# The added row of six gate products, given to TensorE as two rounded parts in a buffer of its own

## What is computed

```
h = rmsnorm_2(x, g_mix[l])
proj = jnp.einsum('bsd,dc->bsc', h, w_in[l])
q_a, k_a, v_a, q_i, k_i, w_i, conv_in, q_m, gate_logits = jnp.split(proj, split_points, axis=-1)
...
gates = jax.nn.sigmoid((gate_logits + b_gate[l]).astype(jnp.float32)).astype(x.dtype)
gates = gates.reshape(B, S, N_BRANCHES, D)
merged = (gates[:, :, 0] * (o_a @ w_br_a[l])
          + gates[:, :, 1] * (o_b @ w_br_b[l])
          + gates[:, :, 2] * (o_m @ w_br_m[l]))
x = x + merged @ w_o[l]
```

## Time and profile before

| | us |
|---|---|
| median of 3 runs | 1756.24 (1755.83 to 1758.96) |
| the profiled execution, its own time | 1757.07 |
| its span, first to last instruction | 1755.0 |
| TensorE busy | 1660.3 |
| VectorE busy | 1216.7 |
| ScalarE busy | 868.3 |
| GpSimd busy | 51.4 |
| mean granted TensorE clock | 0.967 of full |

### The profile page before, as it was taken

How to read it: one execution, slowest core, us unless ns; L and a number is a source line. 1 busy time by engine, 2 the same in 40 slices (tenths; PEclk the granted TensorE clock), 3 DMA queues, 4 the chain that set the end, 5 groups by cost and what they waited for, 6 DMA issues and landing times.

```text
span 1755.0 us, 19937 instructions
## 1 busy us (share of the span) xinstructions
PE 1660.3 (95%) x7889; PEld 1311.8 (75%) x7889; DVE 1216.7 (69%) x1705; ACT 868.3 (49%) x1239; POOL 51.4 (3%) x81
## 2 busy tenths in 40 slices
PE   6999986999999999989999999999989989999997
PEld 2888864778868888658788878766768787787875
DVE  3989976789856765544655555686577558888986
ACT  3445441534444444346544445544354437777774
POOL 1100000001000000000000001000000010000000
PEclk9999997999999999999999999998599989999999
DMA  9998952988749755340666644452022328989993
GB/s 350 375 348 274 323 169 91 360 304 291 249 148 333 251 190 183 133 144 7 235 215 190 193 138 123 162 163 84 26 107 73 120 73 310 353 315 323 333 332 127
DMA packets 200564, 373.78 MB, mean 213 GB/s; under 512 B 8880, under 2 KB 102486, under 8 KB 200464
## 3 DMA queue, kind: packets, MB, share of 16 engines
q1 hardware_dynamic: 186192, 320.48, 53.8%
q0 software_dynamic: 13872, 50.86, 8.3%
q10 hardware_dynamic: 400, 1.10, 0.2%
HBM read 371.36 MB, written 1.05 MB: 212 GB/s over the span
## 4 chain that ended last, share of the span: by engine, by line
PE 84%; DVE 8%; ACT 5%; DMA 1%; issue 1%; SPq 0%; DVEq 0%; ACTq 0%
PE banks L519 23%; PE banks L521 22%; PE banks L520 22%; PE banks L746 2%; PE banks L1258 1%; PE banks L1285 1%; ACT full L718 1%; DVE ul L463 1%; PE banks L1737 1%; PE banks L872 1%; PE banks L2195 1%; PE banks L671 1%; ACT uh L452 1%; PE banks L2240 1%; PE banks L1272 1%
## 5 line engine op out<-in xcount | busy, mean ns | idle before, releaser
L463 DVE TENSOR_TENSOR ul<-raw,uh 128x1024 fp32r<-128x1024 f32 (+2 forms) x548 | 659.6, 1211 | 253.2 <-ACT uh L452 244.9
L452 ACT ACTIVATE uh<-raw 128x1024 fp32r<-128x1024 f32 (+2 forms) x548 | 571.5, 1050 | 488.1 <-PE banks L521 462.5
L519 PE MATMUL banks<-uh,hh 128*128 128x512 f32 (+2 forms) x1280 | 523.5, 409 | 21.8 <-ACT kvm L1123 15.3
L521 PE MATMUL banks<-uh,hl 128*128 128x512 f32 (+2 forms) x1280 | 501.3, 392 | 0.0
L520 PE MATMUL banks<-ul,hh 128*128 128x512 f32 (+2 forms) x1280 | 500.6, 391 | 0.0
L519 PEld LDWEIGHTS banks<-uh,hh 128*128 128x128 f32 x1280 | 244.5, 191 | 85.4 <-ACT kvm L1123 16.2
L520 PEld LDWEIGHTS banks<-ul,hh 128*128 128x128 f32 x1280 | 244.8, 191 | 53.6 <-issue 7.7
L521 PEld LDWEIGHTS banks<-uh,hl 128*128 128x128 f32 x1280 | 244.1, 191 | 51.0
L519 PE MATMUL banks<-uh,bh 128*128 128x512 f32 x528 | 209.3, 396 | 9.3 <-DVE bl L926 4.2
L521 PE MATMUL banks<-uh,bl 128*128 128x512 f32 x528 | 206.0, 390 | 0.0
L520 PE MATMUL banks<-ul,bh 128*128 128x512 f32 x528 | 205.6, 389 | 0.0
(11 more groups left out here) (310 smaller groups left out, 1412.6 us busy)
## 6 DMA issues: line engine op xcount, KB each, us to landing
raw<-in_ffn_w_in SPq DMA_DIRECT2D x176, 512.0 KB, 5.4
raw<-in_w_up SPq DMA_DIRECT2D x64, 1024.0 KB, 5.8
raw<-in_ffn_w_out SPq DMA_DIRECT2D x44, 1024.0 KB, 7.1
arena<-in_ada_w POOLq DMA_DIRECT2D x42, 1024.0 KB, 8.2
raw<-in_w_down SPq DMA_DIRECT2D x32, 1024.0 KB, 5.6
raw<-in_ada_w SPq DMA_DIRECT2D x30, 1024.0 KB, 6.3
raw<-in_w_in SPq DMA_DIRECT2D x22, 1024.0 KB, 5.1
raw<-in_w_mem_kv SPq DMA_DIRECT2D x4, 1024.0 KB, 6.0
```

The source lines that it names most:

```text
L452: act.e.activation(uh[r][:, 0:w], raw[m % NRAW][:, h * w:(h + 1) * w], AF.Copy).then_inc(act_done, ta.put("hi", u))
L463: dve.e.tensor_tensor(ul[r][:, 0:w], raw[m % NRAW][:, h * w:(h + 1) * w], uh[r][:, 0:w].bitcast(F32), ALU.subtract).then_inc(dve_done, tv. ...
L519: pe.e.matmul(o, a, wh, start=s0, stop=False)
L521: mm = pe.e.matmul(o, b, wh, start=False, stop=s1)
```

## The change

GpSimd loads `b_gate` twice, into rows 0 to 5 and 32 to 37 of `adab`. VectorE, in `mix_dve` behind the last low part of the activation (`scaled_dve`), writes a new buffer `gb` of type fp32r: a selecting matrix `gsel` of 38 x 6, zeros, the rounded rows in rows 0 to 5, and in rows 32 to 37 what the rounding left out. `gates_pe` starts each bank with one fp32r matmul over 38 rows, which adds both parts. TensorE no longer waits for the load itself but for VectorE. The second buffer of `pr6` is now `adab`, which is free by then; that makes the arena 516 elements shorter, and `cc` and `st` lose two elements each.

```diff
-ARENA = 11332
+ARENA = 10816
...
-        cc = sb("cc", [P, 48])
+        cc = sb("cc", [P, 46])
...
-        st = sb("st", [P, 280])
+        st = sb("st", [P, 278])
...
+        gb = sb("gb", [P, 520], F32R)
...
-        pr6 = [wide_bufs[2], A(512)]
+        pr6 = [wide_bufs[2], adab[:, :]]
...
+        gsel = gb[0:38, 512:518]
+        gbias = gb[0:38, 0:512]
+
+        def gate_rows_dve(dve):
+            low = gb[32:38, 0:512]
+            dve.wait_ge(loaded("b_gate"), 32)
+            dve.e.tensor_tensor(gsel, ident[0:38, 0:6], ident[0:38, 32:38], ALU.add).then_inc(dve_done, tv.put())
+            dve.e.memset(gb[0:38, 0:512].bitcast(F32), 0.0).then_inc(dve_done, tv.put())
+            dve.own()
+            dve.e.tensor_copy(gbias[0:6, :], adab[0:6, :]).then_inc(dve_done, tv.put())
+            dve.e.tensor_copy(low, adab[32:38, :]).then_inc(dve_done, tv.put())
+            dve.own()
+            dve.e.tensor_tensor(gbias[32:38, :], adab[32:38, :], low.bitcast(F32), ALU.subtract).then_inc(
+                dve_done, tv.put("gb"))
...
-            pe.wait_ge(loaded("b_gate"), 16)
+            pe.wait_ge(dve_done, tv("gb"))
             for b in PAIRS[0]:
                 pe.take(b)
-                pe.e.matmul(PB[b], ident[0:6, j:j + 1].to_broadcast([6, P]), adab[0:6, :], start=True, stop=False)
+                pe.e.matmul(PB[b], gsel[:, j:j + 1].to_broadcast([38, P]), gbias, start=True, stop=False)
...
             scaled_dve(dve, "mix", KD, hh, hl, lambda k: col("g_mix_2", k), lambda k: 0.0)
+            gate_rows_dve(dve)
             dve.e.memset(uT[:, :, 0:30], 0.0).then_inc(dve_done, tv.put("u0"))
...
-            load("b_gate", adab[0:6, :], I["b_gate_2"].rearrange("a (j n) -> (a j) n", n=512))
+            for r in (0, 32):
+                load("b_gate", adab[r:r + 6, :], I["b_gate_2"].rearrange("a (j n) -> (a j) n", n=512))
```

## The result

| | before, us | changed, us |
|---|---|---|
| median | 1755.83 (1752.15 to 1758.96, 5 runs) | 1742.74 (1735.36 to 1743.48, 5 runs) |
| profiled execution, its span | 1757.07, 1755.0 | 1742.52, 1740.7 |
| mean granted TensorE clock of it | 0.967 | 0.971 |

The ratio is 0.9922, 95% interval 0.9896 to 0.9949: faster by 13.1 us at the medians. The prediction said 1744.0, from 1739.5 to 1750.5.

A forecast was written before the change was run, and what follows sets the result against it. TensorE's order was taken as the bound; gains of 3.0 (gates 1 to 3), 4.4 (gate 4), 2.3 (gate 5) and 2.9 (gate 6) sum to 12.6 us, giving 1744 us, 8-in-10 range 1739.5 to 1750.5.

The forecast's parts named there:

- The bound and the path: TensorE holds 84% of the chain that ended last, so time taken from its order is gained unless something replaces it.
- VectorE's five instructions and the load: Near 1074 us: instructions take 2.3 us, hidden while TensorE is busy; the second load lands in time; both cost zero.
- The fp32r pass: Start of each bank: 0.23 us over 38 rows at full clock; a full-clock gate gives 1.2 us.
- Gates 1 to 3: At most 1.8 of 2.4 us reach gate 3 because VectorE holds back the rest; gate 3 adds 1.2: 3.0 us.
- Gate 3's fall: The 3.5 us at half clock behind gate 3, worth 1.7 us, stay because the wait for ScalarE grows.
- Gate 4 and the half clock behind it: At gate 4, shorter passes give 1.7 us and the clock holding behind them 2.7: 4.4 us.
- Gate 5 to gate 6: Gate 5 begins at half clock; passes give 2.9 us, taken as 2.3 since the clock may come back later.
- Gate 6 to the memory heads: Gate 6's passes give 1.2 us and the clock holding behind it 1.7: 2.9 us; VectorE can follow.
- The share of the clock: Of the 12.6 us gain, 4.4 come from the clock holding behind gates 4 and 6, some 8.2 from passes.
- A second HAM failure mode: psum-queue depth-cycling: At the gates, short bank waits swing the clock, so three falls stay: gain 8.2 us, 1748.0; clock-still-falls chance 0.22.
- VectorE as the bound: Before the first heads, VectorE's rotary parts come late: gain 7.2 or 5 us, 1749 to 1751; chance 0.09.
- The memory heads: Rival: these heads run at half clock, 1750.0 us and over, chance 0.05, of which slower than before 0.03.

The follow-up runs named there:

- e5: The changed kernel with VectorE's five new instructions run three times over: 1742.88 us, ratio 0.9943 to the kernel before.
- e8: The changed kernel with the fp32r pass over all 128 rows, 90 of them zeros, instead of 38: 1739.31 us, ratio 0.992 to the kernel before.
- e9: The changed kernel itself, unaltered, run again later: 1741.39 us against 1753.59 for the kernel before, ratio 0.9926.
- e4: The changed kernel with each bank's fp32r pass over only the six rows of high parts, low parts left out: 1746.14 us, ratio 0.9952.
- e11: The six-row fp32r pass (low parts left out) on the changed kernel again, beside the unaltered change on one chip: 1744.32 us against 1741.39, ratio 0.9954.
- e7: The kernel before, with gates 1 and 3 on the other pair of banks and the six-row fp32 passes kept: 1744.60 us, ratio 0.9958.
- e6: The changed kernel with gates 1 and 3 on the other pair of banks, removing waits for ScalarE: 1742.75 us, ratio 0.9938 to the kernel before.
- e10: The changed kernel with both the 128-row fp32r pass and the other pair of banks for gates 1 and 3: 1735.48 us, ratio 0.9902.

## Why the prediction was right

**The bound and the path.** Right. TensorE's order set the end; what was taken at the gates arrived at the end but for 0.6 us.

**VectorE's five instructions and the load.** Right in size, 2.3 us, and in cover; e5 shows about 3 us more cover. The load landed after 4.9 us at the median.

**The fp32r pass.** Right in kind. The first plain matmul came 0.91 us after the first pass, not 0.73: the term was too large by 0.2 us a gate. The weights of the plain matmul load late behind a pass over 38 rows; over 128 rows they load early and part of the 0.2 us comes back (e8), so that is at least part of the reason.

**Gates 1 to 3.** The number is right, by two errors that offset each other. At most 1.8 us of 2.4 was to arrive at gate 3, since VectorE would hold back 0.6. Gate 3 starts 3.33 us earlier, 1.92 without the 1.41 at the start. But gates 1 and 2 gave only 0.92 and 1.00 us, and VectorE held nothing of that back: ScalarE waits 0.70 us for it and TensorE 0.95 for the sigmoid, both as before. The limit itself is real and was just reached. VectorE's 1.83 us of idle time are gone, and with gates that are 0.22 us shorter still (e8) TensorE waits 1.33 us at gate 3 and nothing more arrives.

**Gate 3's fall.** This step failed. I left it in, expecting the wait for ScalarE to grow by 0.6 us, to 1.9, and to bring it. The wait did not grow: it is 0.95 us as before, and some 1.9 us passed between the plain matmuls with the two passes in them. The clock held, in both profiled executions of the change (this one and e9). That gives 1.7 us. With six rows instead of 38 and the same waits the fall is back (e4, e11), so what I lacked was the row count: nothing in the step asks over how many rows the passes run.

**Gate 4, gate 5, gate 6.** Gate 4 and the half clock behind it: 4.4 expected; from gate 4 to the first heads it took 7.71 us and now 3.78, 3.9. Gate 5 to gate 6: 2.3 expected, 16.87 and 14.76, 2.1. Gate 6 to the memory heads: 2.9 expected, 15.94 and 13.32, 2.6.

**The sum.** 12.6 expected, 13.5 found in the profiled pair, less the 0.6 behind the memory heads. The share of the clock was under-sized: 13.6 us at half clock at the gates are gone, worth 6.8, where I counted 4.4; the passes gave 6.7 where I counted 8.2. The two errors offset each other, so that the forecast of 1744 came within 1.3 us is in part luck. The other runs fit this. Runs of the kernel before at a mean clock of 0.971 took 1748.1 to 1749.1 us, those of the change 1742.0 to 1743.5; at 0.972 they took 1748.7 to 1751.8 and 1740.8 to 1743.4: some 6 to 8 us at one clock. The kernel before mostly ran at 0.967 to 0.970, and took up to 1758.6 us at 0.965.

**The rivals.** The rule of the Trainium skill's page TensorE: Matmul & The Clock Gate, section A second HAM failure mode: psum-queue depth-cycling, that frequent short idling between groups of matmuls makes the clock swing, did not decide here: waits of 0.69 to 0.95 us stayed at gates 1 to 4 and 6, and the falls went. But it names half of the cause, since taking the waits away (e7) ended the falls at gates 3 and 4 as well. VectorE as the bound did not come with this change and did with the next step, at the first heads (e6). The memory heads kept the clock.

**Still open.** Why the first heads lose the clock for 44 us and, in two of the kernels, win it back half-way; what sets when it comes back behind gate 5 (1.9 to 9.6 us behind its start), which is worth up to some 4 us; and how often each gate falls, for which one profile a kernel is too little.

## What to carry to other kernels

A small matmul that starts an accumulation can cost more than its passes. Here passes over six rows beside a wait of 0.7 to 0.95 us went with 3.4 to 6.7 us of full work at half clock. Read the granted clock behind such places; if it falls, try to take away either the wait or the empty rows. Zeros in the unused rows cost nothing here. Then look at who is late next: after 13 us from TensorE, VectorE's order was the bound at the first heads, and taking away 3 us more of waiting gained nothing by itself.

## What the runs showed of the hardware that I had not expected

- Rows in use count for the clock: the fp32r pass over 6 rows was 2.9 us slower than over 38 on one chip, with the same length and waits. Rows of zeros seem to count too: fp32 passes over 6, 38 and 128 rows went with three falls, one and none at the gates, though those over 128 were also over sooner.
- A longer wait needs no such pass. Behind 2.28 us (e6) and 3.80 us (e10) of waiting at the first heads the clock fell too, with no added row near.
- The weight load behind a pass over 38 rows starts 0.43 us after that pass's load, behind one over 128 rows 0.10 us after.
- The first heads take 5.50 us each at half clock, 3.4 at full, and can go from one to the other in the middle. In the timeline of e10_two_pairs_128rows:

```profile
1212.14 0.64 PE L1248 MATMUL banks<-ident,arena 128*64 128x128 f32 x2
1217.64 0.64 PE L1248 MATMUL banks<-ident,arena 128*64 128x128 f32 x2
1221.03 0.38 PE L1248 MATMUL banks<-ident,arena 128*64 128x128 f32 x2
...
1224.47 0.38 PE L1248 MATMUL banks<-ident,arena 128*64 128x128 f32 x2
```
